# The hybrid block's first three projections read the residual ahead of the first block's last norm

## The reference

```python
def first_block(x, ...):
    ...                                  # gMLP mixer, MLP 0, chunk attention
    h = h + conv_ffn(rmsnorm(h, f_norm_g[l]), ...)        # MLP 1
    return rmsnorm(h, final_norm_g)

def second_block(x, ...):
    h = x
    for i in range(DEPTH):
        hn = rmsnorm_2(h, attn_norm[i])
        if i % 2 == 0:
            mix = sb_rwkv_mixer(hn, ...)  # proj = hn @ w_in, 3584 columns with padding
        else:
            mix = mla_mixer(hn, ...)
        h = h + mix
        h = h + conv_glu(rmsnorm_2(h, ffn_norm[i]), ...)
        ...                               # per-layer embedding gate
    return rmsnorm_2(h, final_norm)

def rmsnorm(x, g):
    return x * rsqrt(mean(x * x) + EPS) * g
```

## Time and profile before

| what | value |
|---|---|
| three runs, median (range) | 1334.51 us (1334.04 to 1335.72) |
| the profiled execution's own time | 1334.98 us |
| its span, first to last instruction | 1333.2 us |
| PE busy | 98% of the span |
| DVE busy | 69% |
| ACT busy | 57% |
| mean granted TensorE clock | 0.995 of full |

### The profile page before, as it was taken

The page is one execution under the profiler, slowest core; times in us unless marked ns, Lnnn a source line. Parts: engine busy times, 40 slices in busy tenths (PEclk is TensorE's granted clock), DMA queues, the critical chain, the costliest instruction groups (busy, mean ns, idle before and its releaser), DMA issues.

```text
span 1333.2 us, 29291 instructions
## 1 busy us (share of the span) xinstructions
PE 1302.9 (98%) x12212; PEld 1270.5 (95%) x12212; DVE 913.4 (69%) x1294; ACT 756.1 (57%) x979; POOL 44.1 (3%) x37
## 2 busy tenths in 40 slices
PE   8999999999999999999999999999999999999997
PEld 8999999998999999999989899999999889999997
DVE  4779776488479776478654277666478879666456
ACT  6657664367667664367554165555366777554444
POOL 1010000010010000010000010000001001000000
PEclk9999999999999999999999989999999999999999
DMA  8455555555345555535312036553634335555520
GB/s 330 172 208 190 190 189 190 189 190 202 116 159 196 188 187 203 185 136 188 133 34 96 5 103 230 184 188 133 253 120 173 127 130 209 200 189 189 189 96 32
DMA packets 31980, 220.61 MB, mean 165 GB/s; under 512 B 3712, under 2 KB 3840, under 8 KB 6160
## 3 DMA queue, kind: packets, MB, share of 16 engines
q1 hardware_dynamic: 30672, 213.36, 44.7%
q0 software_dynamic: 784, 4.85, 1.1%
q10 hardware_dynamic: 432, 1.05, 0.2%
HBM read 218.20 MB, written 1.05 MB: 164 GB/s over the span
## 4 chain that ended last, share of the span: by engine, by line
PE 84%; DVE 9%; ACT 4%; issue 1%; DMA 1%; POOL 0%; SPq 0%; DVEq 0%; ACTq 0%; POOLq 0%
PE ps L1838 21%; PE ps L1839 20%; PE ps L1840 20%; PE ps L1849 17%; DVE w_lo L1100 3%; PE ps L1844 2%; PE ps L1845 1%; PE ps L1846 1%; ACT w_hi L504 1%; DVE xt L1152 1%; PE ps L2060 1%; DMA raw<-stream 1%; DVE xA L1162 0%; DVE xB L1162 0%; DVE xB L1124 0%
## 5 line engine op out<-in xcount | busy, mean ns | idle before, releaser
L1100 DVE TENSOR_TENSOR w_lo<-raw,w_hi 128x2048 fp32r<-128x2048 f32 x197 | 449.6, 2287 | 147.8 <-ACT w_hi L504 147.4
L504 ACT ACTIVATE w_hi<-raw 128x2048 fp32r<-128x2048 f32 x197 | 375.9, 1913 | 172.9 <-PE ps L1840 167.6
L1838 PE MATMUL ps<-xB,w_hi 128*128 128x256 f32 x1120 | 316.4, 282 | 6.5 <-DVE xB L1662 3.4
L1839 PE MATMUL ps<-xB,w_hi 128*128 128x256 f32 x1120 | 314.0, 280 | 0.0
L1840 PE MATMUL ps<-xB,w_lo 128*128 128x256 f32 x1120 | 314.0, 280 | 0.0
L1838 PEld LDWEIGHTS ps<-xB,w_hi 128*128 128x128 f32 x1120 | 212.1, 189 | 8.1 <-DVE xB L1662 3.6
L1839 PEld LDWEIGHTS ps<-xB,w_hi 128*128 128x128 f32 x1120 | 212.1, 189 | 0.5 <-issue 0.4
L1838 PE MATMUL ps<-xA,w_hi 128*128 128x256 f32 x744 | 211.0, 284 | 1.6 <-ACT ml_v L1016 1.1
L1840 PEld LDWEIGHTS ps<-xB,w_lo 128*128 128x128 f32 x1120 | 211.9, 189 | 0.0
L1840 PE MATMUL ps<-xA,w_lo 128*128 128x256 f32 x744 | 207.8, 279 | 0.0
L1839 PE MATMUL ps<-xA,w_hi 128*128 128x256 f32 x744 | 207.7, 279 | 0.0
(11 more groups left out here) (285 smaller groups left out, 1861.1 us busy)
## 6 DMA issues: line engine op xcount, KB each, us to landing
raw<-stream SPq DMA_DIRECT2D x199, 1024.0 KB, 4.8
raw<-stream SPq DMA_DIRECT2D x4, 512.0 KB, 8.6
at_bias<-rel POOLq DMA_DIRECT2D x1, 2048.0 KB, 8.2
hT<-x_t SPq DMA_DIRECT2D x4, 256.0 KB, 7.7
lora_w<-lora POOLq DMA_DIRECT2D x1, 1024.0 KB, 5.1
out_t<-xt SPq DMA_DIRECT2D x4, 256.0 KB, 2.4
hcon<-hyc POOLq DMA_DIRECT2D x1, 576.0 KB, 4.0
wsT<-wst ACTq DMA_DIRECT2D x1, 512.0 KB, 4.3
```

The source lines that it names most:

```text
L504: nc.scalar.activation(w_hi[c.slot][:], raw[c.slot][:], ACT.Copy).then_inc(hi_made, 1)
L1100: nc.vector.tensor_tensor(w_lo[c.slot][:], raw[c.slot][:], w_hi[c.slot][:].bitcast(F32), ALU.subtract).then_inc(lo_made, 1)
L1838: nc.tensor.matmul(out, wh, xh, start=start, stop=False, skip_group_check=True)
L1839: nc.tensor.matmul(out, wh, xl, start=False, stop=False, skip_group_check=True)
```

## The change

The final norm is no longer done at the seam. The first three hybrid chunks read `hT` as MLP 1 leaves it, with `hy_gain = f a` as their gain. ACT squares `hT` and also `hT * f` (two more operations for each quarter, into `slot2` and `slot3`); DVE folds the second set with three additions; PE sums both in the pair, now between its k steps 6 and 7 instead of 4 and 5. ACT takes the first root (`fin_rs`), DVE makes r1 squared times the second mean, ACT takes the second root, and DVE multiplies the two. `hT` is rewritten to h r1 f only later, in DVE's stream between the evacuations of products 10 and 14 of the RWKV part; `add_quarter` of the hybrid block's output waits for that. The final norm's sums on PE and their `keep_clock` matmuls are gone, and so is one load of ACT's table.

```diff
 # ACT
             ffn(1, N_FF1)
-            square_norm(N_FIN1)
             c0 = C0["hy"]
             for b in range(4):
                 square(N_HY, b)
+                for k in (2 * b, 2 * b + 1):
+                    last = nc.scalar.activation(slot[2 + k // 4][:, k % 4, :], hT[:, k, :], ACT.Square, scale=col("fin1", k))
+                last.then_inc(fin_sq, 1)
             split_hi(Chunk(c0).ahead())
-            root_norm(N_HY)
+            act.wait_ge(ss_summed, N_HY + 1)
+            inverse_root(fin_rs[:], half(4, 0), D, fin_made)
+            act.wait_ge(fin_mean, 1)
+            inverse_root(rs[:], rs[:], 1, rs_made)
             round_x(OUT_HY, xA)
...
 # DVE, at the end of ffn(1)
+                if n + 1 == N_HY:
+                    dve.wait_ge(fin_sq, 4)
+                    for i in (2, 3):
+                        own.mark(nc.vector.tensor_tensor(slot[i][:, 0:2, :], slot[i][:, 0:2, :], slot[i][:, 2:4, :], ALU.add))
+                    own.wait()
+                    nc.vector.tensor_tensor(slot[2][:, 0:2, :], slot[2][:, 0:2, :], slot[3][:, 0:2, :],
+                                            ALU.add).then_inc(fin_folded, 1)
                 split_lo(Chunk(d0 + PAIRS - 1).ahead())
...
 # DVE, behind MLP 1's norm and behind ffn(1)
             scale_x(OUT_FF1, xA, "f_norm1")
+            link(nc.vector.tensor_tensor(hy_gain[:], col("fin1", 0, KD), col("at_norm0", 0, KD), ALU.mult))
             ffn(1, N_FF1)
-            root(N_FIN1)
-            for k in range(KD):
-                ins = nc.vector.scalar_tensor_tensor(out=hT[:, k, :], in0=hT[:, k, :], scalar=col("fin1", k), in1=rs[:],
-                                                     op0=ALU.mult, op1=ALU.mult)
...
-            for b in range(4):
-                rest_early(N_HY, b)
-            fold_squares(N_HY)
-            split_lo(Chunk(c0).ahead())
+            dve.wait_ge(fin_made, 1)
+            link(nc.vector.scalar_tensor_tensor(out=rs[:], in0=half(4, 1), scalar=1.0 / D, in1=fin_rs[:], op0=ALU.mult,
+                                                op1=ALU.mult))
+            nc.vector.tensor_tensor(rs[:], rs[:], fin_rs[:], ALU.mult).then_inc(fin_mean, 1)
+            split_lo(Chunk(c0).ahead())
...
             root(N_HY)
+            link(nc.vector.tensor_tensor(rs[:], rs[:], fin_rs[:], ALU.mult))
             scale_x(OUT_HY, xA, "at_norm0")
...
 # DVE, in the RWKV part
             split_lo(Chunk(c0 + 12).ahead())
+            for k in range(KD):
+                nc.vector.scalar_tensor_tensor(out=hT[:, k, :], in0=hT[:, k, :], scalar=col("fin1", k), in1=fin_rs[:],
+                                               op0=ALU.mult, op1=ALU.mult).then_inc(fin_scaled, 1)
             with_eye(14, 7, -1)
...
 # PE
             ffn(1, N_FF1, OUT_FF1, xA)
-            keep_clock(10, 3)
-            sum_quarters(N_FIN1, range(4))
...
-                    early_pair(N_HY, Chunk(c0), Chunk(c0 + 1), 5)
+                    early_pair(N_HY, Chunk(c0), Chunk(c0 + 1), 7)
...
 # POOL
-            add_squares(N_FIN1)
             pool.wait_ge(h_updated, 16)
             pool.dma_start(hcon[:], hyc[:, 2 * P:]).then_inc(hy_landed, 16)
```

More of the change, by code:

```diff
@@ L83 @@
 SCALED_AT = {n: sum(c for m, (_, c) in EARLY.items() if m < n) for n in EARLY}
-FOLDED = tuple(n for n in range(12) if n not in (N_FIN1, N_FIN2))
-ADDED_BY = {n: sum(2 if m in FOLDED else 1 for m in range(n)) for n in range(12)}
+FOLDED = tuple(range(N_FIN2))
+ADDED_BY = {n: sum(2 if m in FOLDED else 1 for m in range(n)) for n in range(11)}
 FOLD_AT = {n: i for i, n in enumerate(FOLDED)}
 FINAL_XT = 8 * 10
-FILL = (3, 9)
 GATE_BANK = (4, 6, 7, 5)
@@ L143, in build @@
         rs = sb("rs", [P, T])
+        hy_gain = sb("hy_gain", [P, KD])
         with ExitStack() as f:
@@ L264, in build @@
         rs_made = sem("rs_made")
+        fin_sq, fin_folded, fin_made, fin_mean, fin_scaled = [
+            sem(n) for n in ("fin_sq", "fin_folded", "fin_made", "fin_mean", "fin_scaled")]
         xt_made = sem("xt_made")
@@ L344, in product_bank, with early_gain @@
             return (2 * i + b) % 3 if i < BESIDE else 2 * ((i + 2) % 4) + b
+        def early_gain(n, k):
+            return hy_gain[:, k:k + 1] if n == N_HY else col(EARLY[n][0], k)
         def early_tile(n):
@@ L1151, in scale_x @@
                 for k in range(KD):
-                    nc.vector.scalar_tensor_tensor(out=xt[:, k, :], in0=hT[:, k, :], scalar=col(gain, k), in1=rs[:],
+                    nc.vector.scalar_tensor_tensor(out=xt[:, k, :], in0=hT[:, k, :],
+                                                   scalar=early_gain(N_HY, k) if o == OUT_HY else col(gain, k), in1=rs[:],
                                                    op0=ALU.mult, op1=ALU.mult).then_inc(xt_made, 1)
@@ L1858, in keep_clock, with sum_quarters @@
                     plain(ps[:, bank, 0:P], ones, ones)
-            def sum_quarters(n, quarters, idle=True):
+            def sum_quarters(n, quarters):
                 for b in quarters:
@@ L1883, in sum_folded @@
                 plain(half(4, 0), ones, xt[:, 6, :], True, False)
-                plain(half(4, 0), ones, xt[:, 7, :], False, True).then_inc(ss_summed, 1)
+                last = plain(half(4, 0), ones, xt[:, 7, :], False, True)
+                if n == N_HY:
+                    pe.wait_ge(fin_folded, 1)
+                    plain(half(4, 1), ones, slot[2][:, 0, :], False, False)
+                    last = plain(half(4, 1), ones, slot[2][:, 1, :], False, True)
+                last.then_inc(ss_summed, 1)
             def wide_chunk(c, bank, x, ready=None, between={}, blocks=2):
@@ L2505, in _ @@
             keep_clock(12)
-            sum_quarters(N_FIN2, (2, 3), idle=False)
+            sum_quarters(N_FIN2, (2, 3))
 def _cols(v):
```

22 lines of the change are left out of this document (9 added, 13 removed).

## The result

The changed kernel takes 1339.04 us (median of 7 runs, 1335.34 to 1342.23) against 1334.51 us before (7 runs, 1332.87 to 1336.27): a ratio of 1.0031, 95% interval 1.0017 to 1.0044. It is slower by 0.2 to 0.4%, and 7.4 us above the forecast of 1331.6. Yet the seam itself went as forecast.

A forecast was written before the change was run, and what follows sets the result against it. PE was taken to bound the kernel, busy for 98% of the span. 4.92 us from an earlier hy+4, less 2.0 lost to the clock, gave 2.92 us off 1334.51: 1331.6 us, range 1329.5 to 1334.2.

The forecast's parts named there:

- the seam: Between MLP 1 and the hybrid chunks: hy+4 starts 4.92 us earlier, 2.92 us kept after the clock's loss.
- The lane of DVE: DVE's operations from the roots to w_lo of hy+4: they move 2.89 us earlier and decide when hy+4 starts.
- PE's 9.39 us: PE at the seam: without the separate final norm, hy+2 starts 9.39 us earlier.
- The cover of 1.2 us: Slack at the seam's pair: the folds and w_lo of hy+2 are ready about 1.2 us before PE needs them.
- the rival of a late feed: At the seam, ACT, DVE or POOL delay the second sum beyond its slack: 1332.6 to 1334.1 us, chance 0.17.
- the clock: Behind PE's 4.4 us idle time before hy+4: the granted clock falls and costs 2.0 us, between 1.2 and 2.7.
- The rival in which it stays low: Clock stays low behind hy+4: through hy+4, LoRA products and hy+5 it costs 8 us, for 1337.6; chance 0.08.
- the rewrite: Eight moved DVE operations, 3.26 us, fit into DVE's 3.66 us idle time before product 14's evacuation, 0.5 us to spare.
- The tiny `hy_gain` product costs about 0.2 us [...]: nothing: On DVE behind MLP 1's norm: the product takes about 0.2 us while PE works without waiting, so it adds nothing.
- Memory traffic is unchanged: For the whole kernel: no term was charged for memory traffic.
- the one on the slower side: The rival of a clock that stays low behind hy+4, up to 1337.6 us, chance 0.08.
- anything else that is slower: Remainder without a named mechanism or place: any other slower outcome, chance 0.02.

The follow-up runs named there:

- e9: Changed kernel with hy_gain ahead of all tiles, plus 19 filler matmul pairs on PE in the idle time before hy+4: 1329.90 us, ratio 0.9968 to the kernel before.
- e5: Changed kernel with hy_gain laid out ahead of all tiles instead of between rs and xB: 1332.93 us against 1334.37 for the kernel before, ratio 0.9992.
- e1: Kernel before with only an unused 32-byte tile where the changed kernel has hy_gain: 1339.75 us against 1334.59, ratio 1.0042.
- e6: e5 with an unused tile of 96 bytes between rs and xB, single execution: 1351.8 us.
- e7: e5 with an unused tile of 160 bytes between rs and xB, single execution: 1334.8 us.
- e2: Changed kernel with 96 unused bytes behind hy_gain, so that x is moved by 128 bytes: 1341.89 us, ratio 1.0048 to the kernel before.
- e8: e5 with an unused tile of 224 bytes between rs and xB, single execution: 1356.4 us.
- e11: e5 with an unused tile of 16 bytes between rs and xB, which really moved x by 32 bytes, single execution: 1336.8 us.
- e12: e5 with an unused tile of 192 bytes between rs and xB, single execution: 1342.8 us.
- e4: Kernel before with 32 unused bytes ahead of all tiles, every distance between tiles kept: 1334.20 us, ratio 1.0000.

## Why the prediction was wrong

**Right: the seam.** Counted from MLP 1's end, the second sum began after 10.76 us (10.47 forecast), `scale_x` after 16.32 (16.18), hy+4 after 28.68 (28.40) behind 4.17 us of idle time (4.4), and the LoRA products after 35.82 (36.0). The lane of DVE decided, not PE's 9.39 us. The cover of 1.2 us held (PE has no idle place from the pair's start to hy+4), and the rival of a late feed did not come.

**Right: the clock.** It fell once behind the gap and rose again after 3.4 us. It cost 1.5 us by e9's hy+4, where I had 2.0. The fall was a safe guess: all eight traces with the seam's gap left open (3.9 to 4.6 us) show it. The rival in which it stays low, the one that would have made the kernel slower, did not come.

**Right: the rewrite.** It took 3.25 us and ended 0.49 us ahead of the evacuation of product 14; I had 3.26 and 0.5. The working there mixes 710.16 and 710.08 for the end of `w_lo`; from 710.16 the cover would be 0.4.

**Wrong: "The tiny `hy_gain` product costs about 0.2 us [...]: nothing" and "Memory traffic is unchanged".** The step prices `hy_gain` as an instruction and never as a tile, and takes it that matmuls whose code is unchanged keep their speed. Its 32 bytes moved every x tile against the weights, and the spacing of the matmuls rose by 1.1 ns. At 7 us for each ns that is some 8 us, an estimate. Stretches with streamed weights give a part back (8 matmuls more in 20 to 60 us are 0.9 us), and e5, which differs from the kernel after in the place of that tile alone, is 6.1 us faster (5.2 by the ratios; e1, the tile without the change, costs 5.2 to 5.6). So 6.1 us of layout less the 1.6 by which e5 lies below 1334.5 are the 4.5 us that the kernel after lost. No rival covered it: the one on the slower side had another mechanism, only the 0.02 for "anything else that is slower" was left for it, and the range ended at 1334.2.

**Left.** With the layout repaired the gain is 1.4 us in the median (interval: 2.5 us gained to 0.3 lost), less than the seam's 3.1 us. Part of it is clock: 0.9938 against 0.9955 in the runs of before beside it, and in the traces five low stretches of 3.4 us against 10.2 us in all before. In e5's profiled execution PE also stood for 1.76 us in the RWKV part (up to 712.58) without a wait that the profile names. The traces of e6 and e7 have the same 1.76 us; the kernel after, e2, e8, e11 and e12 have 0.55 there. What decides it stays open.

## What to carry to other kernels

A new tile is an edit to all tiles that are laid out behind it: compare the addresses (here a tile takes a multiple of 32 bytes, whatever it asks for), and put small new tiles where they don't move matmul operands against each other, or try a few paddings on purpose. If PE's instruction count in a stretch of unchanged code differs at the same clock, look at the layout before looking at the edit. Price a shorter critical path by the engine whose lane is next (here DVE's `w_lo`), and fill the idle time that this opens on PE.

## What the runs showed of the hardware

- The spacing of back-to-back 128x256 float32 matmuls depends on the distance in SBUF between the streamed tile and the weights' tile. Moved in steps of 32 bytes, it is 116.7 ns at the distance of before and 256 bytes further on, and 120.0 at worst (64 and 224 bytes), 24 us of this kernel. It is the same with ACT and DVE idle.
- At some distances the stream has two states, 113.3 and 117.8 ns (moves of 32 and 160 bytes), or 116.7 and 117.8 (move 0, e4), which hold for over 110 us and were seen to switch where other matmuls come between. The Trainium skill, SBUF — State Buffer, section "Operand start alignment", treats the start address as a question of legality and says that its runs timed nothing; here addresses that are all legal differ by 1.8% in time.
- The granted clock fell in stretches of 3.4 or 6.8 us. The one at the seam cost 1.5 us, and half of 3.4 us is 1.7. The same idle time does not always bring it: 3.3 to 3.4 us near 765 were followed by a low clock in 16 of 20 traces. Runs of one kernel differ by the number of such stretches: in e9 a mean clock of 0.998 went with 1327.4 and 1328.0 us, and 0.995 to 0.996 with 1329.5 to 1331.1.
